# A tuned decoder trunk on one core: root mean squares by a square of ones, ScalarE's root and VectorE's Newton step

## The reference

```python
def rms_norm(x, g):
    xf = x.astype(jnp.float32)
    y = xf * lax.rsqrt(jnp.mean(xf * xf, axis=-1, keepdims=True) + EPS)
    return (y * g.astype(jnp.float32)).astype(x.dtype)

def layer_norm(x, g, b):
    xf = x.astype(jnp.float32)
    mu = jnp.mean(xf, axis=-1, keepdims=True)
    xc = xf - mu
    y = xc * lax.rsqrt(jnp.mean(xc * xc, axis=-1, keepdims=True) + EPS)
    return (y * g.astype(jnp.float32) + b.astype(jnp.float32)).astype(x.dtype)

# every layer, with h = rms_norm(x, norm_mix):
x = x + 0.5 * swiglu_ffn(rms_norm(x, norm_ffn[l, 0]), w_in, w_out)
x = x + mixer(h)      # conv_module with layer_norm inside, or attention
x = x + 0.5 * swiglu_ffn(rms_norm(x, norm_ffn[l, 1]), w_in, w_out)
# between the layers: kv = rms_norm(x, kv_norm) @ w_kv; at the end: rms_norm(x, norm_final)
```

## Time and profile before

| | us |
|---|---|
| median of 3 runs | 2233.27 |
| lowest and highest of them | 2231.94, 2236.64 |
| the profiled execution | 2235.43 |
| its span, first to last instruction | 2233.4 |
| TensorE busy | 2140.6 (96%) |
| VectorE busy | 943.0 (42%) |
| ScalarE busy | 619.4 (28%) |
| GpSimd busy | 501.6 (22%) |
| mean granted TensorE clock | 0.97 |

### The profile page before, as it was taken

One profiled execution on the slowest core, in us unless ns is written; L12 is line 12 of the kernel. 1 busy time (PEld: TensorE's weight loads), 2 busy tenths in 40 slices (PEclk: granted clock), 3 DMA queues, 4 the chain that ended last, 5 costly groups with the idle time before them and its releaser, 6 DMA issues.

```text
span 2233.4 us, 40029 instructions
## 1 busy us (share of the span) xinstructions
PE 2140.6 (96%) x16556; PEld 2034.3 (91%) x16556; DVE 943.0 (42%) x1149; ACT 619.4 (28%) x929; POOL 501.6 (22%) x309
## 2 busy tenths in 40 slices
PE   7999999999899999999999999999867999999997
PEld 7999999877599999999999999999645599999997
DVE  4333333698743333333343333333598243333222
ACT  4222222332432222222132222222334132222221
POOL 1323301000033332102203333112342023332211
PEclk9999999999999999999999999999867899999998
DMA  5233332211023333322343233333441323323331
GB/s 167 87 92 94 103 91 81 83 52 53 12 86 95 89 90 101 104 87 81 114 110 94 88 91 104 95 91 116 142 142 67 113 76 94 92 86 97 104 91 38
DMA packets 347164, 206.26 MB, mean 92 GB/s; under 512 B 6115, under 2 KB 338276, under 8 KB 346940
## 3 DMA queue, kind: packets, MB, share of 16 engines
q1 hardware_dynamic: 339044, 191.31, 28.7%
q10 hardware_dynamic: 6856, 7.53, 1.0%
q0 software_dynamic: 1184, 6.28, 0.8%
HBM read 198.52 MB, written 7.53 MB: 92 GB/s over the span
## 4 chain that ended last, share of the span: by engine, by line
PE 91%; DVE 6%; ACT 1%; issue 1%; POOL 1%; DMA 0%; POOLq 0%; DVEq 0%; ACTq 0%; SPq 0%
PE ps_all L497 82%; PE ps_all L519 3%; DVE pr L1253 2%; PE ps_all L673 1%; DVE mx L1244 1%; DVE s_dec L1319 1%; PE ps_all L506 1%; PE ps_all L560 1%; PE ps_all L570 1%; PE ps_all L594 1%; PE ps_all L635 1%; DVE at_n L1256 0%; POOL inv L1454 0%; PE ps_all L618 0%; DVE w_lo L1029 0%
## 5 line engine op out<-in xcount | busy, mean ns | idle before, releaser
L497 PE MATMUL ps_all<-xg_hi,w_hi 128*128 128x260 f32 x3456 | 704.6, 285 | 14.2 <-DVE xg_lo L1039 11.3
L793 ACT ACTIVATE w_hi<-raw 128x1024 fp32r<-128x1024 f32 (+1 forms) x296 | 334.7, 1131 | 1369.6 <-PE ps_all L497 1368.3
L497 PE MATMUL ps_all<-xg_hi,w_lo 128*128 128x260 f32 x3456 | 699.1, 284 | 0.0
L497 PE MATMUL ps_all<-xg_lo,w_hi 128*128 128x260 f32 x3456 | 698.1, 284 | 0.0
L497 PEld LDWEIGHTS ps_all<-xg_hi,w_hi 128*128 128x128 f32 x3456 | 536.9, 190 | 16.6 <-DVE w_lo L1029 13.0
L497 PEld LDWEIGHTS ps_all<-xg_hi,w_lo 128*128 128x128 f32 x3456 | 535.5, 189 | 0.0
L497 PEld LDWEIGHTS ps_all<-xg_lo,w_hi 128*128 128x128 f32 x3456 | 534.7, 189 | 0.0
L1029 DVE TENSOR_TENSOR w_lo<-raw,w_hi 128x1024 fp32r<-128x1024 f32 (+1 forms) x296 | 399.1, 1348 | 269.8 <-ACT w_hi L793 269.8
L497 PE MATMUL ps_all<-h_hi,w_hi 128*128 128x260 f32 x1664 | 341.1, 285 | 5.7 <-DVE h_lo L1193 5.7
L497 PE MATMUL ps_all<-h_hi,w_lo 128*128 128x260 f32 x1664 | 338.6, 283 | 0.0
L497 PE MATMUL ps_all<-h_lo,w_hi 128*128 128x260 f32 x1664 | 338.1, 283 | 0.0
(11 more groups left out here) (158 smaller groups left out, 1226.9 us busy)
## 6 DMA issues: line engine op xcount, KB each, us to landing
raw<-w_in SPq DMA_DIRECT2D x176, 512.0 KB, 3.7
raw<-w_out SPq DMA_DIRECT2D x64, 704.0 KB, 4.2
raw<-c_in SPq DMA_DIRECT2D x16, 512.0 KB, 3.8
raw<-w_kv SPq DMA_DIRECT2D x16, 512.0 KB, 3.7
page<-cache_k SPq DMA_DIRECT2D x16, 512.0 KB, 4.5
page<-cache_v SPq DMA_DIRECT2D x14, 512.0 KB, 4.7
raw<-c_out SPq DMA_DIRECT2D x8, 512.0 KB, 3.7
raw<-w_q SPq DMA_DIRECT2D x8, 512.0 KB, 3.6
```

The costliest lines, as they stand in the source:

```text
L497: mm = nc.tensor.matmul(unit[slot][:, s, :], w[:, c % 2, k * P:(k + 1) * P], m[:, s * HALF:(s + 1) * HALF], start=kk == 0 and i == 0, stop ...
L793: nc.scalar.activation(w_hi[:, c % 2, 0:w], raw[:, c, 0:w], ACT.Copy).then_inc(hi_made, 1)
```

## The change

The column sums, the power on GpSimd and the spread are gone. `variance` is now two matmuls with the 128 x 128 square of ones as stationary side and the halves of `acc` as moving side, so the mean squares come out on every partition, 128 x 520 in PSUM. ScalarE takes the square root of the sums plus EPS into `rstd` (`root`). VectorE takes the reciprocal y of that, and then one Newton step from the sums themselves, v = mean square + EPS: y (1.5 - 0.5 v y y), in three passes, each of which waits for the one ahead. `acc` serves as scratch.

In the layer norm the root reads the sums of `mean` at once. At the start the root stands between the squares and the constants on ScalarE.

```diff
-                pe.wait_ge(acc_copied, 1)
-                for i, b in enumerate(BLOCKS):
-                    mm = nc.tensor.matmul(ps_all[:, 6, i:i + 1], acc[:, b:b + P], cst[:, C_ID:C_ID + 1], start=True, stop=True)
                 mm.then_inc(var_done, 1)
-                spread(made + 1)
...
             def variance(sums, free):
...
-                for i, b in enumerate(BLOCKS):
-                    mm = nc.tensor.matmul(ps_var[:, i:i + 1], acc[:, b:b + P], ones_d[:, 0:1], start=True, stop=True)
+                for s in range(2):
+                    mm = nc.tensor.matmul(ps_stat[:, s, :], ones_d[:, :], acc[:, s * HALF:(s + 1) * HALF], start=True, stop=True)
                 mm.then_inc(var_done, 1)
-
-            def spread(made):
-
-                pe.wait_ge(inv_made, made)
-                for i, b in enumerate(BLOCKS):
-                    half, at_b = divmod(b, HALF)
-                    mm = nc.tensor.matmul(ps_stat[:, half, at_b:at_b + P], inv[:, i:i + 1].broadcast_to([P, P]),
-                                          cst[:, C_ID:C_ID + P], start=True, stop=True)
-                mm.then_inc(spread_done, 1)
...
+            def root():
+
+                roots[0] += 1
+                act.wait_ge(var_done, roots[0])
+                nc.scalar.activation(halves(rstd[:, :]), ps_stat, ACT.Sqrt, bias=eps_c[:, 0:1]).then_inc(rooted, 1)
...
-            def rms(squares=ps_var):
-
+            def rms():
+
+                step = 3 * made[0]
                 made[0] += 1
-                dve.wait_ge(var_done, made[0])
-                nc.vector.tensor_scalar(var[:, :], squares, EPS, None, ALU.add).then_inc(var_read, 1)
-                dve.wait_ge(spread_done, made[0])
-                nc.vector.tensor_copy(halves(rstd[:, :]), ps_stat).then_inc(rstd_made, 1)
+                dve.wait_ge(rooted, made[0])
+                nc.vector.reciprocal(rstd[:, :], rstd[:, :]).then_inc(newton, 1)
+                dve.wait_ge(newton, step + 1)
+                nc.vector.scalar_tensor_tensor(halves(acc[:, :]), ps_stat, EPS, halves(rstd[:, :]), ALU.add, ALU.mult
+                                               ).then_inc(newton, 1)
+                dve.wait_ge(newton, step + 2)
+                nc.vector.scalar_tensor_tensor(acc[:, :], acc[:, :], -0.5, rstd[:, :], ALU.mult, ALU.mult).then_inc(newton, 1)
+                dve.wait_ge(newton, step + 3)
+                nc.vector.scalar_tensor_tensor(rstd[:, :], acc[:, :], 1.5, rstd[:, :], ALU.add, ALU.mult).then_inc(rstd_made, 1)
                 dve.wait_ge(rstd_made, made[0])
...
-                dve.wait_ge(sq_used, KD)
-                nc.vector.tensor_copy(halves(acc[:, :]), ps_stat).then_inc(acc_copied, 1)
-                rms(ps_all[:, 6, 0:6])
+                rms()
```

More of the change, by code:

```diff
@@ L185, in trunk @@
         minus_half = place("minus_half", [P, 6])
+        eps_c = place("eps_c", [P, 1])
         assert cursor[0] <= nc.sbuf_usable_end, cursor[0]
@@ L229, in trunk @@
         ps_stat = ps_all[:, 4:6, 0:HALF]
-        ps_var = ps_all[:, 4, 0:6]
         ps_rot = ps_all[:, 6:8, 0:HALF]
@@ L249, in trunk @@
         sq_used = sem("sq_used")
-        acc_copied = sem("acc_copied")
         summed = sem("summed")
@@ L253, in trunk @@
         var_done = sem("var_done")
-        var_read = sem("var_read")
-        inv_made = sem("inv_made")
-        spread_done = sem("spread_done")
+        rooted = sem("rooted")
+        newton = sem("newton")
         rstd_made = sem("rstd_made")
@@ L377, in trunk @@
         TURN_AT = SCORES_AT + 4
-        BLOCKS = tuple(s * HALF + at for s in range(2) for at in (0, P, HALF - P))
         def shares(m):
@@ L535, in layer_norm @@
                     pe.wait_ge(squared, 2 * KD + m + 1)
-                    mean(m, sq[:, m % 2, :], ps_stat).then_inc(sq_used, 1)
-                pe.wait_ge(acc_copied, 1)
-                for i, b in enumerate(BLOCKS):
-                    mm = nc.tensor.matmul(ps_all[:, 6, i:i + 1], acc[:, b:b + P], cst[:, C_ID:C_ID + 1], start=True, stop=True)
+                    mm = mean(m, sq[:, m % 2, :], ps_stat)
+                    if m < KD - 1:
+                        mm.then_inc(sq_used, 1)
                 mm.then_inc(var_done, 1)
-                spread(made + 1)
             def variance(sums, free):
                 if not free:
-                    pe.wait_ge(inputs, N_IN)
-                    pe.wait_ge(const_done, 2)
+                    pe.wait_ge(const_done, 3)
                 pe.wait_ge(summed, sums)
@@ L742, in body @@
                         else:
-                            chunk(ph, g, c, {2: lambda: spread(made + 1)} if opening and c == 1 and fresh(ph) else ())
+                            chunk(ph, g, c)
                         r = 4 * g + c - 1
@@ L801, in x_hi @@
                 nc.scalar.activation(xg_hi[:, m, :], x[:, m, :], ACT.Copy, scale=gain(s, m)).then_inc(xg_hi_made, 1)
+            roots = [0]
+            def root():
+                roots[0] += 1
+                act.wait_ge(var_done, roots[0])
+                nc.scalar.activation(halves(rstd[:, :]), ps_stat, ACT.Sqrt, bias=eps_c[:, 0:1]).then_inc(rooted, 1)
             act.wait_ge(vec_in, 16)
@@ L815, in _ @@
                 nc.scalar.activation(sq[:, m % 2, :], x[:, m, :], ACT.Square).then_inc(squared, 1)
+            root()
             act.wait_ge(inputs, N_IN)
@@ L994, in _ @@
             for ph in phases:
+                if fresh(ph) and ph is not phases[0]:
+                    root()
                 if ph.kind == "up":
@@ L1360, in _ @@
             nc.gpsimd.memset(minus_half[:, :], -0.5).then_inc(const_done, 1)
+            nc.gpsimd.memset(eps_c[:, :], EPS).then_inc(const_done, 1)
             sums, squares = [KD], [KD]
@@ L1401, in load_for @@
                     pool.dma_start(kT[:, :, :], k_d).then_inc(in_kt, 16)
-            def conv_in(ph):
-                squares[0] += KD
-                rms()
             def rotary(ph):
@@ L1454, in power @@
                 return nc.gpsimd.tensor_tensor(inv[0:rows, 0:n], var[0:rows, 0:n], minus_half[0:rows, 0:n], ALU.pow)
[L1456 to L1461, removed]
             for ph in phases:
                 load_for(ph)
-                if fresh(ph):
-                    rms()
                 if ph.kind == "up":
@@ L1469, in _ @@
                 elif ph.kind == "conv_in":
-                    conv_in(ph)
+                    squares[0] += KD
                 elif ph.kind in ("k", "q"):
```

## The result

| | us |
|---|---|
| before, median of 6 runs (2228.82 to 2236.64) | 2231.85 |
| with the change, median of 6 runs (2238.95 to 2243.55) | 2242.38 |
| ratio, with its 95% interval | 1.004 (1.0028 to 1.0051) |
| the profiled execution with the change, its span | 2240.92, 2239.1 |

The change costs 10.5 us, 6.2 to 11.4 by the interval; 11.7 was forecast. First the chain that ended last, share of the span by engine; it answers to the earlier trace rows.

The account below looks back on a forecast made before the run. TensorE, holding 91% of the chain that ended last, was taken as the bound. Openings +2.1, clock +8.5, layer norm -1.2, end +0.1 and start +2.2 sum to +11.7 on 2233.3: 2245 us, range 2216 to 2258.

Parts of the forecast that it names:

- The slack: Before chunk 2 of a phase's opening, 1.4 us between w_lo's end and TensorE's need; forecast to be used up.
- TensorE's gain: At each opening TensorE gives 2.97 us of work and takes 0.98, a gain of 1.99 us.
- the clock: One drop of TensorE's granted clock behind each of five openings, +8.5 us; rival that it holds: 2236 us, chance 0.13.
- R: Time of VectorE's reciprocal of 520 columns in each root, taken as 3.0 us, with ends 0.7 and 5.3.
- the fast end: Rival of a fast reciprocal in every root, near 0.7 us: a time of 2218 us, chance 0.26.
- Three openings: conv_in, second up and last up: chunk 2 starts 0.41 us later each, plus 1.7 us of low clock each.
- k and q: Two of the five phase openings, forecast like the others: 0.41 us later and 1.7 us of low clock each.
- the five openings: Roots opening conv_in, second up, k, q and last up: +2.1 us together (-9.5 to +13.6), without the clock's drops.
- Start: First root, where VectorE waits for lambda's exp before the reciprocal: w_lo's end later, +2.2 us (-0.1 to +4.5).
- layer norm: From the last mean to the first use of rstd: -1.2 us (-3.5 to +1.1).
- end: Final norm, up to the start of the final pass: +0.1 us (-2.2 to +2.4).
- The table loads: Rival: ScalarE's table loads lie on each root's path, 10.2 us more, a time of 2255 us, chance 0.06.

## Why the prediction was right, and where it was not

**The mechanism held.** The slack was used up, TensorE's gain was waited away and the clock fell. Taking the reciprocal away turned 10.5 us of loss into 16.6 of gain. With R at 0.7, its low end, the forecast had 2218 us, and this kernel, with no reciprocal at all, has 2215.

**R** was taken as 3.0, the middle between 0.7 and 5.3, and is 3.40: 0.4 us too little, and eight times that is 3.2. The equal durations of one and two columns in the earlier trace rows were no evidence for the fast end. From 156 ns for one column to 3404 for 520 it is 6.26 ns a column, and yet the two columns took no longer than the one. The Trainium skill's repeat count of 8 (VectorE: DVE Perf Modes, "First, the fixed hardware budget"), read as cycles at 0.96 GHz, gave an estimate of 4.4 us, too long by 1.0: the slope would be six such cycles a column. That the divide is iterative no run here shows.

**The other passes** were 0.756 with a handover of 0.05 and are 0.70 with 0.035, so three take 2.2 us and not 2.42; the root is 0.70 and not 0.61. With R's 0.4 that makes the chain 0.3 too short. TensorE's own gain, forecast at 1.99 an opening, is 2.19 where nothing is waited for.

**Three openings**: 0.41 later was forecast, 0.65 came; a low clock of 1.7 us each, 1.6 came.

**k and q** are the step that failed. I took the five openings as alike, and counted one drop of the clock for each. Before the change they are alike to the end of chunk 1 only, 8.8 to 8.9 us behind the start of the sums. What stands there is chunk 2 at three of them, but at k and q a rotation, which needs `t_gate` and not `w_lo` and fills the time in which the others stand idle. Forecast was 0.41 + 1.7 each. Measured is 9.33 us from sums to chunk 2 (1048.33 to 1057.66) against 9.56 (1041.85 to 1051.41), so -0.2 each and no low clock: 4.7 us less in all. The run with two more passes shows where this sparing ends.

**Start** +2.3 (forecast +2.2), **layer norm** -1.0 (-1.2), **end** +0.4 (+0.1).

**The sum** by measured parts is 2.3 + 3 × (0.65 + 1.6) - 0.4 - 1.0 + 0.4 = 8.1 us. The medians differ by 10.5 with an interval from 6.2, the two profiled spans by 5.7. The profiled execution of before was 3.6 us above its median and the other 1.5 below, so the two traces understate what the medians say. Between the two traces other places count too. From the sums of k to those of q it is 1.4 us less with the change, from there to the last up 2.0 less, where the openings explain 0.2 each. One place: ahead of the last rotation of k, TensorE idles 3.05 and 3.06 us, and the four passes of the rotation took 2.07 us before the change, at low clock, and 1.11 after it. The rest of these stays open. The forecast of 11.7 lies 3.6 above the parts: k and q were 4.7 too dear, everything else together 1.1 too cheap. That it also lies close to the medians' 10.5 is partly luck.

**The table loads** as a rival are refuted: a gain of 2.0 where 10 would have been. The row of a load is 1.28 us, and at the layer norm the root follows 0.02 us behind it. The Trainium skill has some 2.7 us for a switch of the set (ScalarE: Activation LUTs, "Table sets: the hidden batching unit"), and this trace shows no more than the load's 1.28. Its rule to batch by set would have bought one load here, the one ahead of lambda's exp: with the root behind the exp, the start was shorter by 1.3 us.

## What to carry to other kernels

A step that is cheap for the bounding engine is no gain if the chain behind it outgrows its cover: work out when the bounding engine next needs something, and add up the chain to that point for every place apart, since places that look alike may need different things next. Where all partitions hold the same row, an operation costs the whole width again; the reciprocal of 520 columns takes as long as five passes, and ScalarE's one over the root spares it at the price of the plain root. How exact that is without a Newton step behind it, no run here measures. An idle time of two to three microseconds of TensorE cost more than itself here, through the clock behind it. And once a wait is gone, look for the next one: here it was the load of the convolution's state.

## What was not expected of the hardware

- VectorE's reciprocal takes 3404 ns for 128x520 and 156 ns for 128x1, but 155 ns for 128x2: the cost per column doesn't show in the shortest ones.
- Idle times of 1.40 us at k and q had no low clock behind them; 2.19, 2.72, 2.86 and 4.84 had. The length of the low stretch doesn't follow that of the idle time: at conv_in it was 3.4 us behind 2.72, 6.4 behind 4.18 (two more passes), and 3.2 behind 6.16 (two reciprocals). Behind 3.05 us near the end of k the clock was low at once in the trace of before, and in that of the changed kernel, behind 3.06, only 1.3 us later.
- Matmuls that nobody reads, put in the idle time, kept the granted clock at 1.00: 7.4 us gained.
- ScalarE's one over the root takes 696 ns for 128x520 from PSUM, the same as its root.
